# Output weights between the last eight DMA transposes, and three strips of the first output tiles between the last mixing products

## The reference, cut to what matters

```python
h = _rmsnorm(x, pre_norm[l])
proj = h @ w_in[l]
...
y = jnp.concatenate([_merge(o_a), _merge(o_b), _merge(o_c), _merge(o_m)], axis=-1)
y = y * jax.nn.silu(gate)
x = x + _rmsnorm(y @ w_out[l], post_norm[l])
```

## Time and profile before

| | us |
|---|---|
| median of 3 runs | 2732.6 (2725.76 to 2734.64) |
| the profiled execution | 2734.1, its span 2732.2 |
| TensorE busy | 2448.7 (90% of the span) |
| VectorE, ScalarE, GpSimd busy | 1803.1, 1616.6, 1340.9 |
| mean granted clock of TensorE | 0.973 of full speed |

### The profile page before, as it was taken

How to read it: one execution, slowest core, us unless ns; L and a number is a source line. 1 busy time by engine, 2 the same in 40 slices (tenths; PEclk the granted TensorE clock), 3 DMA queues, 4 the chain that set the end, 5 groups by cost and what they waited for, 6 DMA issues and landing times. The chain is left out here.

```text
span 2732.2 us, 73492 instructions
## 1 busy us (share of the span) xinstructions
PE 2448.7 (90%) x27422; PEld 1669.4 (61%) x27422; DVE 1803.1 (66%) x4993; ACT 1616.6 (59%) x4437; POOL 1340.9 (49%) x2128
## 2 busy tenths in 40 slices
PE   5799999988899999888999998889999997599998
PEld 4576666665666666666766766567666665444443
DVE  7658988765479887665699976646998775311111
ACT  5457765567667755576677555766785557511121
POOL 6414457766434576674245766752456677400000
PEclk9899999999999999999999999989999999799999
DMA  6346874498758943898589537994886368963331
GB/s 204 91 99 116 148 141 98 83 172 152 160 103 142 158 105 79 159 161 158 102 152 154 118 77 148 156 169 92 157 143 126 82 128 151 187 207 97 104 108 47
DMA packets 942750, 357.38 MB, mean 131 GB/s; under 512 B 768292, under 2 KB 927148, under 8 KB 942380
## 3 DMA queue, kind: packets, MB, share of 16 engines
q1 hardware_dynamic: 935800, 334.83, 62.7%
q0 software_dynamic: 6592, 17.83, 2.4%
HBM read 89.22 MB, written 35.23 MB: 46 GB/s over the span
## 5 line engine op out<-in xcount | busy, mean ns | idle before, releaser
L1507 POOL TENSOR_TENSOR rows<-rows 128x512 f16<-128x512 f32 (+3 forms) x864 | 861.1, 1010 | 808.3 <-ACT rows L1442 804.2
L1271 PE MATMUL job<-wt,big 128*128 128x128 f16 x10752 | 672.9, 221 | 9.3 <-DVE planes L1518 4.5
L1271 PE MATMUL job<-big,wt 128*128 128x512 f16 x2688 | 662.7, 384 | 18.5 <-DVE planes L1518 6.7
L1271 PEld LDWEIGHTS job<-wt,big 128*128 128x128 f16 x10752 | 630.0, 99 | 59.6 <-DVE planes L1518 11.4
L1442 ACT CAST rows<-rows 128x512 f16<-128x512 f32 (+3 forms) x864 | 465.1, 547 | 254.7 <-DVE rows L1589 123.4
L1332 PE MATMUL mixed<-values,rows 128*128 128x64 f16 (+1 forms) x8544 | 446.2, 202 | 119.0 <-DMA rows<-rows 89.2
L1332 PEld LDWEIGHTS mixed<-values,rows 128*128 128x128 f16 x8544 | 391.4, 100 | 254.6 <-DMA rows<-rows 132.3
L1454 ACT ACTIVATE rows<-rows,neg_max 128x512 f32<-128x512 f32 (+3 forms) x704 | 447.0, 637 | 89.4 <-DVE neg_max L1564 88.4
L1556 DVE TENSOR_SCALAR_CACHE_REDUCE rows<-scores 128x512 f32<-128x512 f32 (+3 forms) x704 | 400.0, 588 | 148.0 <-POOL rows L1507 125.4
L1317 PE MATMUL scores<-stack 128*128 128x512 f16 (+3 forms) x1600 | 438.1, 351 | 54.5 <-DVE rows L1556 44.3
L1271 PEld LDWEIGHTS job<-big,wt 128*128 128x128 f16 x2688 | 249.0, 99 | 277.9 <-issue 20.6
(11 more groups left out here) (160 smaller groups left out, 3000.8 us busy)
## 6 DMA issues: line engine op xcount, KB each, us to landing
stack<-planes SPq DMA_DIRECT2D x160, 192.0 KB
ws<-w_in SPq DMA_DIRECT2D x56, 512.0 KB, 4.6
y_halves<-y_out_halves SPq DMA_DIRECT2D x64, 256.0 KB, 3.3
rows<-rows SPq DMA_TRANSPOSE x864, 3.3
rows<-x SPq DMA_DIRECT2D x16, 512.0 KB, 5.7
temps<-w_out POOLq DMA_DIRECT2D x64, 128.0 KB, 3.2
out_weight_halves<-temps POOLq DMA_DIRECT2D x64, 128.0 KB, 3.6
planes<-y_halves SPq DMA_DIRECT2D x8, 1024.0 KB, 8.7
```

Source lines behind the costliest of these rows:

```text
L1271: last = nc.tensor.matmul(dst, lhs, rhs, start=(k0 == 0 and q == 0), stop=(k1 == KT and q == len(pairs) - 1))
L1507: nc.gpsimd.tensor_tensor(halves_of(tau, 1, w), scored(plan.chunk_at(g, m, k0), 0, w), halves_of(tau, 0, w), ALU.subtract).then_inc(low_po ...
```

## The change

SyncE no longer issues the 16 weight loads behind its last transpose. `out_weights` is called after each of the last eight transposes, with its number `at`. Call 0, behind the first of them, waits for all that the loads need and loads the first columns of y. Every call loads two strips. Call 7 also loads the next columns of y. TensorE's loop over strips becomes a function `out_strip(k)`. Strips 0, 1 and 2 are run behind the mixing products of chunks `LAST_TAU - 4`, `LAST_TAU - 2` and `LAST_TAU`. The others stay behind the list. The flag `skip_group_check=True` only concerns the build, since the accumulations into the score banks are now interleaved with those of the mixing products. The values computed are the same.

```diff
@@ -1067,6 +1067,8 @@
         out_banks = [(s_bank[0], s_bank[1]), (s_bank[2], s_bank[3]), (j_bank[0], j_bank[1])]
         LAST_READ = max(job[0] for job in plan.job_of.values())
         LAST_TAU = max(tau for cuts in plan.t_chunks.values() for tau, *_ in cuts)
+        LAST_CUTS = len(plan.t_chunks[plan.n_steps - 1])
+        EARLY = {LAST_TAU - 4 + 2 * k: k for k in range(3)}
         N_G = plan.n_steps
         KINDS = [UNIT[t].kind for t, _ in plan.steps]
         SOFT = [g for g in range(N_G) if KINDS[g] != "stick"]
@@ -1181,22 +1183,24 @@
                     else:
                         sp.dma_start(dst[64:128], src[:, 3:0:-1, :]).then_inc(stacked[c], 16)
 
-                def out_weights():
-
-                    for c in range(NC):
-                        sp.wait_ge(stacked[c], STACKED[-1])
-                    sp.wait_ge(y_stored[0], STORE * (Y_GROUPS // 2 - 1))
-                    src = y_dram[:, :, 0:2 * P].rearrange("h (k f) s -> f h k s", f=P)
-                    for h in range(2):
-                        sp.dma_start(yl[0][:, h], src[:, h]).then_inc(y_in[0], 16)
-                    sp.wait_ge(wo_stored, 16 * WO_PIECES)
-                    sp.wait_ge(j_full, LAST_READ + 1)
-                    for k in range(YT):
+                def out_weights(at):
+
+                    if at == 0:
+                        for c in range(NC):
+                            sp.wait_ge(stacked[c], STACKED[-1])
+                        sp.wait_ge(y_stored[0], STORE * (Y_GROUPS // 2 - 1))
+                        src = y_dram[:, :, 0:2 * P].rearrange("h (k f) s -> f h k s", f=P)
+                        for h in range(2):
+                            sp.dma_start(yl[0][:, h], src[:, h]).then_inc(y_in[0], 16)
+                        sp.wait_ge(wo_stored, 16 * WO_PIECES)
+                        sp.wait_ge(j_full, LAST_READ + 1)
+                    for k in range(at * YT // LAST_CUTS, (at + 1) * YT // LAST_CUTS):
                         sp.dma_start(wo[:, :, k], wo_dram[:, :, k]).then_inc(wo_in[k], 16)
-                    split_done(sp, LAST_TAU)
-                    src = y_dram[:, :, 2 * P:4 * P].rearrange("h (k f) s -> f h k s", f=P)
-                    for h in range(2):
-                        sp.dma_start(yl[1][:, h], src[:, h]).then_inc(y_in[1], 16)
+                    if at + 1 == LAST_CUTS:
+                        split_done(sp, LAST_TAU)
+                        src = y_dram[:, :, 2 * P:4 * P].rearrange("h (k f) s -> f h k s", f=P)
+                        for h in range(2):
+                            sp.dma_start(yl[1][:, h], src[:, h]).then_inc(y_in[1], 16)
 
                 for op, *args in plan.orders["sp"]:
                     if op == "stacks":
@@ -1230,8 +1234,8 @@
                         sp.dma_start_transpose(
                             turned[tau % PT_RING][:, 0:2 * tiles * P].rearrange("p (k q) -> p k q", q=P),
                             split[tau % SPLIT_RING][:, 0:2 * tiles * P]).then_inc(turned_in[tau % PT_RING], 16)
-                        if tau == LAST_TAU:
-                            out_weights()
+                        if tau > LAST_TAU - LAST_CUTS:
+                            out_weights(tau - LAST_TAU + LAST_CUTS - 1)
                     if op == "store":
                         g = args[0]
                         yg = g // 4
@@ -1337,6 +1341,21 @@
                                 skip_group_check=True)
                     last.then_inc(pv_done, 1)
 
+                def out_strip(k):
+                    if k == 0:
+                        pe.wait_ge(s_free, soft_count(plan.last_chunk[len(UNIT) - 1]))
+                        pe.wait_ge(y_in[0], 32)
+                    pe.wait_ge(wo_in[k], 16)
+                    for i in range(2):
+                        for n in range(2):
+                            for a, b in ((0, 0), (0, 1), (1, 0)):
+                                last = nc.tensor.matmul(
+                                    out_banks[i][n][:, :], yl[0][:, a, k, i * P:(i + 1) * P],
+                                    wo[:, b, k, n * BANK:(n + 1) * BANK], start=(k == 0 and a == b == 0),
+                                    stop=(k == YT - 1 and a == 1), skip_group_check=True)
+                        if k == YT - 1:
+                            last.then_inc(out_full, 1)
+
                 for op, *args in plan.orders["pe"]:
                     if op == "part":
                         part(*args)
@@ -1344,25 +1363,16 @@
                         scores(args[0], *args[1])
                     if op == "mix":
                         mix(args[0], *args[1], first=args[2], end=args[3])
+                        if args[1][0] in EARLY:
+                            out_strip(EARLY[args[1][0]])
                     if op == "y":
                         g = args[0]
                         bank = bank_of(plan.y_job[g])
                         pe.wait_ge(post_step, POST_AT[g] + POST[KINDS[g]])
                         nc.tensor.transpose(bank[:, 0:P], y_f[:, g % 2, :], ident[:, :]).then_inc(j_full, 1)
 
-                pe.wait_ge(s_free, soft_count(plan.last_chunk[len(UNIT) - 1]))
-                pe.wait_ge(y_in[0], 32)
-                for k in range(YT):
-                    pe.wait_ge(wo_in[k], 16)
-                    for i in range(2):
-                        for n in range(2):
-                            for a, b in ((0, 0), (0, 1), (1, 0)):
-                                last = nc.tensor.matmul(
-                                    out_banks[i][n][:, :], yl[0][:, a, k, i * P:(i + 1) * P],
-                                    wo[:, b, k, n * BANK:(n + 1) * BANK], start=(k == 0 and a == b == 0),
-                                    stop=(k == YT - 1 and a == 1))
-                        if k == YT - 1:
-                            last.then_inc(out_full, 1)
+                for k in range(len(EARLY), YT):
+                    out_strip(k)
 
             @block.scalar
             def _(act):
```

## The result

The changed kernel takes 2739.35 us in the median of ten runs, the kernel before 2732.05 us in its ten: ratio 1.0033, interval 1.0021 to 1.0045. It is slower by 7.3 us. Six of its ten executions took 2736 to 2740 us and four 2743 to 2745; the profiled one is of the six. The profiled execution took 2738.3 us (span 2736.5), 4.2 us more than that of before (2734.1).

What follows compares the result with a forecast made beforehand. It took the DMA engines as the bound first, TensorE after. The last transpose's later landing put the end 14.6 us later: 2734.1 + 14.6 = 2748.7, and 2747.2 us because the profiled execution was 1.5 above the median; range 2736 to 2759.

Steps and rivals of the forecast that it cites:

- The path that sets the end: The end moves with the third output tile's first matmul, which follows the last transpose's landing: 14.6 us later.
- turn 0: The last DMA transpose, of chunk LAST_TAU (turn n is that of LAST_TAU-n); predicted to land at 2405.8 us.
- Turn 7 to the landing of turn 6: First two of the last eight transposes: the second lands behind the y load and two weight loads, 1.8 us after these.
- The round: Two weight loads and one transpose in SyncE's queue: 2 x 1.36 + 1.8 = 4.5 us, six times.
- From T to the third output tile: T is when turn 0 lands; last product, 14 strips, slow start and transposition of y then take 39.9 us.
- My rival on the clock: Early strips bring TensorE to full speed before the last transpose lands: 2.2 us less, 2746.5; no separate chance given.
- slow start of 2.16 us: Time TensorE loses at low clock when the output strips begin; the prediction kept it at 2.16 us.
- S: Time from the start of the first of the last eight transposes to the third output tile's first matmul: 69.2 us before.
- rival of cheap turns: Each transpose behind copies costs 1.0 us, a round 3.7 us: +8.8 us, 2742.9; chance 0.18.
- my own round of 4 to 5.5 us: The prediction's main case for two loads and a transpose, with or without the clock; chance 0.52.
- The early strips hide and cost nothing: Strips 0 and 1 fill gaps of about 1 to 4.5 us; one product may be 0.7 us late, not turn 0.
- a gain has no route because 14 strips stay behind T: No gain above 3 us, since 14 strips follow the landing of turn 0; faster by over 0.3% had chance 0.03.

Runs made afterwards that it cites:

- e1: The change with no strip run early, all 16 behind the transposition of y; ratio 1.0065 to the kernel before.
- e4: The change with one weight load instead of two in front of each turn, the other nine behind the last transpose; ratio 1.0014 to the kernel before.
- e11: The change, but SyncE waits for the last transpose to land before issuing the last two weight loads and next y load; one execution, S 78.0 us, no ratio.
- e2: The change's early strips kept, but all weight loads and the y load back behind the last transpose; ratio 1.0005 to the kernel before.
- e10: The change with SyncE's queue kept and 14 early strips, two behind each of the last seven mixing products; ratio 0.9973 to the kernel before.
- e8: The change with the 16 weight loads issued by ScalarE on its own DMA queue, the y load left on SyncE; ratio 1.0054 to the kernel before.
- e5: The change with the two halves of the first y load moved up behind the transposes 20 and 16 from the end; ratio 1.0029 to the kernel before.

## Why the prediction was right in direction and too high in size

- **The path that sets the end.** Right. The end moved with the first matmul of the third output tile, and this with turn 0. e1 shows the loads as the cause, with the last product where the change has it and no strips.
- **Turn 7 to the landing of turn 6: 16.8 us predicted, 14.8 measured.** Load 1 was to land 15.0 us after turn 7 and landed after 13.8 (2367.78 + 6.4): the load of y and load 0 took 1.2 us less than before, and SyncE was held by load 0 for 3.2 us and not for the 5.07 of the earlier trace rows. The other 0.8 us is turn 6, which landed 1.0 us behind load 1 and not 1.8.
- **The round: 4.5 us predicted; 23.0/6 = 3.8 us measured, and 3.6 in all but the last.** This is the mis-sized term. I took 1.8 us for a turn behind copies, the middle of 1.0 and 2.7. In a full queue it is 3.6 - 2 x 1.36 = 0.9, as e4 confirms (2.2 - 1.36 = 0.8). With it the two differences are accounted for: seven turns at 0.9 us less are -6.3 us, the pause of the DMA engines in the last round (see e11) is +1.4. The long gap of the earlier trace rows was most likely latency in a queue that had been nearly empty; I had named that reason and given it too little weight, and no run tests it by itself. The Trainium skill ("DMA: Bandwidth & Descriptors", section "Latency and other measured facts") gives 261 GB/s for DMA transposes with a non-contiguous middle dimension and about 350 to 400 GB/s for contiguous ones; it does not speak of a full queue, as my prediction had it. That makes an estimated 1.0 or 0.7 us a turn, and the measured 0.8 to 0.9 us lies between; the measured number decides.
- **From T to the third output tile: 39.9 us predicted, 37.3 measured** (2398.16, where turn 0 landed, to 2435.44). My rival on the clock came true: the slow start of 2.16 us fell away, and the last product ran at full clock too. It fell away with a last wait of 3.48 us; with one of 4.45 us (e11) it came back.
- **The sum.** -2.0 - 4.1 - 2.6 = -8.7 us, and 14.6 - 8.7 = 5.9, against 5.8 in S. The outcome is the rival of cheap turns (+8.8) together with that of the clock (-2.2), 6.6 us. I had given cheap turns a chance of 0.18, and my own round of 4 to 5.5 us, with 0.52, did not come. The mechanism was right; that the time lies in the range is owed to its lower end, 2736, which takes in the cheap turns.
- **The early strips hide and cost nothing.** Right by e2, where nothing is lost but the wait for load 0.
- **That a gain has no route because 14 strips stay behind T.** Right for this change, and it names what was missing: e10 leaves four strips behind the last product instead of 14 and is faster than before.

## What to carry to other kernels

A transfer queued between others that an engine waits for makes all of them late by its bytes, also on another queue. So count what the waiting engine can do with the early data before it arrives at the end of the row: here two early loads a round cost 2.7 us a round, and three early strips gave back only part of it, while 14 paid for it. When data is moved ahead, move its use ahead with it.

## What the runs showed of the hardware that was not expected

- A DMA transpose of 0.26 MB costs about 0.9 us in a full queue, though its own way from start to landing is 3.3 us. Two single places with copies ahead showed 1.0 and 2.7 us, up to 1.8 us more.
- Weight loads on ScalarE's DMA queue slow the transposes on SyncE's: turn 6 took 12.8 us to land and 9.9 us of issue, with ten loads issued ahead of it, against 6.7 and 2.0 with all in one queue and two loads ahead (e8 and the change).
- With turn 0 issued and not yet landed, the DMA engines paused for 1.3 to 1.4 us (23 to 40 GB/s instead of about 350) in the last round of the change, of e5 and of e11.
- The same work met TensorE's full clock in one run (2.75 us for strip 2, after 3.48 us of idle time) and half of it in another (4.83 us, after 4.45 us).
